# Second attention of a two-layer encoder: two heads turned in one transpose, rows spread by DMA

## The reference

```python
q, k, v = jnp.split(h @ w_in, 3, axis=-1)          # 16 heads of 64
q = rmsnorm(q.reshape(B, S, N_HEADS, HEAD_DIM), q_g)
k = rmsnorm(k.reshape(B, S, N_HEADS, HEAD_DIM), k_g)
# every chunk of 64 queries sees its own chunk and the 8 before it
logits = jnp.einsum('bqhd,bkhd->bhqk', q_c, k_c) * scale + bias
logits = jnp.where(valid, logits, -jnp.inf)
p = jax.nn.softmax(logits, axis=-1)
o = jnp.einsum('bhqk,bkhd->bqhd', p, v_c)
h = h + m @ w_out
```

## Time and profile before

| | us |
|---|---|
| median of 3 runs | 2830.57 |
| lowest, highest | 2827.06, 2833.55 |
| profiled execution, its own time | 2832.51 |
| span in its trace | 2830.7 |
| busy in the span: PE, PEld | 2737.7, 2378.0 |
| busy in the span: DVE, ACT, POOL | 1406.7, 1124.8, 952.1 |
| unit loop of the second attention | 1727 to 1996 in the trace |

### The profile page before, as it was taken

The page is one execution under the profiler, slowest core; times in us unless marked ns, Lnnn a source line. Parts: engine busy times, 40 slices in busy tenths (PEclk is TensorE's granted clock), DMA queues, the critical chain, the costliest instruction groups (busy, mean ns, idle before and its releaser), DMA issues. The chain is left out here.

```text
span 2830.7 us, 38924 instructions
## 1 busy us (share of the span) xinstructions
PE 2737.7 (97%) x14678; PEld 2378.0 (84%) x14678; DVE 1406.7 (50%) x2300; ACT 1124.8 (40%) x2409; POOL 952.1 (34%) x695
## 2 busy tenths in 40 slices
PE   7799999999999999999999999999989999999999
PEld 6599889887788888888889998989868888888887
DVE  5888766631544444445441114656244544444444
ACT  5677666642322222222245556777223222222221
POOL 2124433102332233222344445665133233232222
PEclk9899999999999999999999999999999999999999
DMA  5100000101111111111121100002111111111111
GB/s 173 45 26 21 27 9 9 64 24 51 47 55 50 44 44 52 52 44 44 52 93 52 61 23 7 28 13 81 31 53 51 45 44 52 51 45 51 44 52 60
DMA packets 38756, 132.44 MB, mean 47 GB/s; under 512 B 4240, under 2 KB 12608, under 8 KB 36960
## 3 DMA queue, kind: packets, MB, share of 16 engines
q1 hardware_dynamic: 38624, 130.68, 14.1%
HBM read 122.22 MB, written 13.69 MB: 48 GB/s over the span
## 5 line engine op out<-in xcount | busy, mean ns | idle before, releaser
L367 PE MATMUL banks<-XH,WH 128*128 128x512 f32 x1408 | 440.8, 394 | 19.2 <-POOL WL L314 12.6
L314 POOL TENSOR_TENSOR WL<-WR,WH 128x1024 fp32r<-128x1024 f32 x132 | 330.0, 2507 | 380.7 <-ACT WH L260 380.7
L367 PE MATMUL banks<-XL,WH 128*128 128x512 f32 x1408 | 441.2, 395 | 0.0
L367 PE MATMUL banks<-XH,WL 128*128 128x512 f32 x1408 | 438.3, 393 | 0.0
L275 ACT ACTIVATE Y<-U,CONVB,CONVW 128x1024 f32<-128x1024 f32 x88 | 109.5, 1244 | 639.8 <-DVE U L415 639.8
L367 PEld LDWEIGHTS banks<-XH,WH 128*128 128x128 f32 x1408 | 265.3, 189 | 78.9 <-POOL WL L314 13.4
L367 PEld LDWEIGHTS banks<-XH,WL 128*128 128x128 f32 x1408 | 266.1, 189 | 60.9
L415 DVE TENSOR_TENSOR U<-banks,RB 128x1024 f32<-128x1024 f32 x88 | 107.8, 1225 | 418.4 <-PE banks L367 403.5
L367 PEld LDWEIGHTS banks<-XL,WH 128*128 128x128 f32 x1408 | 266.2, 189 | 58.1
L322 POOL TENSOR_TENSOR AL<-Y,AH 128x1024 fp32r<-128x1024 f32 x44 | 106.2, 2413 | 611.8 <-ACT AH L283 611.8
L405 DVE TENSOR_TENSOR XT<-XT,banks 128x1024 f32<-128x1024 f32 x176 | 214.6, 1219 | 164.5 <-PE banks L383 164.5
(11 more groups left out here) (257 smaller groups left out, 5535.2 us busy)
## 6 DMA issues: line engine op xcount, KB each, us to landing
WR<-in_ffn SPq DMA_DIRECT2D x132, 512.0 KB, 3.5
QWR<-in_qkv SPq DMA_DIRECT2D x8, 1536.0 KB, 6.5
XT<-in_xT SPq DMA_DIRECT2D x16, 512.0 KB, 7.5
OWR<-in_w_o SPq DMA_DIRECT2D x16, 512.0 KB, 3.4
QWR1F<-in_qkv SPq DMA_DIRECT2D x4, 1536.0 KB, 6.6
spill<-XT SPq DMA_DIRECT2D x8, 512.0 KB, 10.8
XT<-spill SPq DMA_DIRECT2D x8, 512.0 KB, 7.1
outT<-XT SPq DMA_DIRECT2D x8, 512.0 KB, 2.6
```

Source lines behind the costliest of these rows:

```text
L314: pool.tensor_tensor(WL[:, ch % RING, :], WR[:, ch % RING, :], WH[:, ch % RING, :].bitcast(F32), ALU.subtract).then_inc(w_lo, 1)
L367: mm = pe.matmul(u[:, h * HALF:(h + 1) * HALF], w[:, ch % RING, db * P:(db + 1) * P], x[:, db, h * HALF:(h + 1) * HALF], start=(db == 0 an ...
```

## The change

Two heads are turned by one transpose of their natural 128 columns (q pair, k pair), so TQ holds head 0 in partitions 0 to 63 and head 1 in 64 to 127. ACT copies these 2 x 128 columns to a new buffer HC. Four DMAs per tile, issued by SP, bring each head's 64 rows into both halves of HT. POOL's split waits for the DMAs; its doubling is gone for the 56 tiles of the loop (tiles 0 to 7 keep it). ACT's copy of a tile waits for the DMAs of the tile two before.

```diff
@@ band_phase
+        HC = u.take("HC1", [P, 2, 2 * PAIR], F32)
...
-        q_copied, tq_free, out_high = sem("q_copied"), sem("tq_free"), sem("out_high")
+        h_landed = [sem("h_even"), sem("h_odd")]
+        tq_free, out_high = sem("tq_free"), sem("out_high")
@@ sync
+            def spread(t):
+
+                n, pairs = t - TT, HT[:, t % 2, :].rearrange("p (b h n) -> p b h n", b=2, h=2)
+                if n >= 2:
+                    sp.wait_ge(k_ready, n - 1)
+                sp.wait_ge(tq_free, round_of_tile(t) - TT + 1)
+                for h in range(2):
+                    head = HC[h * HD:(h + 1) * HD, t % 2, :].rearrange("p (b n) -> p b n", b=2)
+                    for to in range(2):
+                        sp.dma_start(pairs[to * HD:(to + 1) * HD, :, h, :], head).then_inc(h_landed[t % 2], 16)
+
+            for t in range(TT, 2 * TT):
+                spread(t)
             for k in range(2, GROUPS):
                 sp.wait_ge(max_done, UNITS * (k - 1))
                 sp.dma_start(BB[:, k % 2, :, PW - W:PW], near[k]).then_inc(b_landed[k % 2], 16)
...
                     for ch in range(c.chunks[1].count):
                         sp.dma_start(c.chunks[1].W[:, ch, :], stream[ch]).then_inc(c.chunks[1].landed, 16)
+                for t in range(k * TT, (k + 1) * TT):
+                    spread(t)
@@ scalar
             def heads_copy(t, r):
                 act.wait_ge(turned, r + 1)
-                if t >= TT + 2:
-                    act.wait_ge(k_ready, t - TT - 1)
-                act.activation(HT[:, t % 2, 0:2 * P], TQ[:, 0:2 * P], ACT.Copy, scale=c.HGAIN[:, 2:3]).then_inc(q_copied, 1)
-                act.activation(HT[:, t % 2, 2 * P:4 * P], TQ[:, 2 * P:4 * P], ACT.Copy,
+                n = t - TT
+                if n >= 2:
+                    act.wait_ge(h_landed[t % 2], 64 * (n // 2))
+                act.activation(HC[:, t % 2, 0:PAIR], TQ[:, 0:PAIR], ACT.Copy, scale=c.HGAIN[:, 2:3])
+                act.activation(HC[:, t % 2, PAIR:2 * PAIR], TQ[:, PAIR:2 * PAIR], ACT.Copy,
                                scale=c.HGAIN[:, 3:4]).then_inc(tq_free, 1)
@@ gpsimd
-                pool.wait_ge(q_copied, n + 1)
+                pool.wait_ge(h_landed[t % 2], 64 * (n // 2 + 1))
...
-                pool.wait_ge(tq_free, round_of_tile(t) - TT + 1)
...
-            doubled(TT)
-            doubled(TT + 1)
...
                     split(t)
-                    if t + 2 < TILES:
-                        doubled(t + 2)
@@ tensor
+            def heads_compact(t, r):
+                pe.wait_ge(normed, t + 1)
+                wait_seat(r)
+                for j in range(2):
+                    mm = pe.transpose(TQ[:, j * PAIR:(j + 1) * PAIR], tile(t)[:, j * PAIR:(j + 1) * PAIR], c.IDF[:])
+                mm.then_inc(turned, 1)
...
-                    heads(tile_of(g), rounds_before(g))
+                    heads_compact(tile_of(g), rounds_before(g))
```

## The result

The changed kernel takes **2837.57 us** (median of 12 runs, 2831.86 to 2842.44), the kernel before, run beside it, 2831.05 us (12 runs, 2827.06 to 2833.99). The ratio is 1.0025, 95% interval 1.0017 to 1.0032: slower by 6.5 us, where 6.4 us less was forecast; 2837.57 lies above the range of 2810 to 2834. The profiled execution took 2842.44 us (the slowest of the twelve; span 2840.6, clock 0.985), that of before 2832.51 (span 2830.7, clock 0.990).

The account below looks back on a forecast made before the run. TensorE, busy 262.4 of 269 us, was taken to bound the second attention's unit loop. Terms -12.9 - 4.5 - 2.0 + 13.0 = -6.4 us gave 2824.2 us against a median of 2830.6; range 2810 to 2834.

Parts of the forecast that it names:

- A: Likeliest case: gains less one group 7 stall, as one queue's last transfers wait for the first; 2824.2 us, chance 0.54.
- transposes: Second attention's unit loop: two transposes fewer per tile, 0.23 us for each of 56 tiles, -12.9 us.
- group 4's burst: Before group 4, BB and two OWR, a quarter of the bytes, make rows land about when due: 0.
- group 7's stall: TensorE waits for late rows in group 7: 10.9 us, restart 0.5, lower clock 1.6, together +13.0 us.
- bank waits and late doubling: Loop: output transpose's waits for the TQ bank, -4.5 us; transposes at 1905.85 late for POOL's doubled rows, -2.0 us.
- ACT's copies: Copies shrink from 256 to 128 columns, a pair taking 0.47 instead of 0.84 us, freeing TQ earlier: -4.5 us.
- The DMAs at price 0: Each loop tile's four row transfers land about 3.5 us after the copies, soon enough for POOL's split: price 0.
- Rival D: Four DMAs served one after the other, landing after 6.8 to 10.4 us, set the loop's pace: 2859 us, chance 0.08.
- The place where it costs: Before group 7, tile 56's rows queue behind BB, XT and WR; TensorE stalls at an output transpose: +10.9 us.
- The clock: After group 7's stall the granted clock stays low, priced from the idle stretch around 1728 to 1730: +1.6 us.
- Rival B: Tile 56's transfers slip past the load or it drains faster: only the gain remains, 2811.2 us, chance 0.16.
- rival C: DVE and ACT set the pace in short units, savings come back as other waits: 2830.7 us, chance 0.18.

Follow-up runs that it names:

- no_spread: The changed kernel without HC and the row DMAs, ACT copying into HT, rows not reaching both halves (output not the reference's): 2812.64 us, ratio 0.9938 to before.
- load_behind: The changed kernel with the eight XT and two WR transfers issued behind group 7's tiles instead of ahead: 2820.63 us, ratio 0.9969 to before.
- half_dmas: The changed kernel with only the two DMAs per tile that cross halves, own-half rows left out (output not the reference's): 2828.48 us, ratio 1.0001 to before.
- three_deep: The changed kernel with three buffers of HT and HC instead of two, all four DMAs per tile kept: 2826.61 us, ratio 0.9984 to before.

## Why the prediction was wrong

The mechanism forecast as the likeliest case, A, is the one that happened: the transposes are saved, the DMAs of rows are free in an undisturbed group, and the load ahead of tile 56's rows makes one large stall. The sign was wrong, because the terms of the sum were mis-sized, all in one direction: above all group 4's burst, put at 0 and worth 5.3 us, and group 7's stall with its clock, put at 13.0 and measured at 18.75. Forecast -6.4 us, measured in the loop +8.1:

| term | forecast | measured |
|---|---|---|
| transposes | -12.9 | -12.3 (0.22 a tile, 56 tiles) |
| bank waits and late doubling | -6.5 | -4.5 (the rest of no_spread's 16.8) |
| group 7's stall, restart and clock | +13.0 | +18.75 |
| group 4's burst | 0 | +5.3 |
| start of the loop and the rest | not named | +0.8 |
| sum | -6.4 | +8.1 |

*Transposes.* 0.24 us a pair against 0.46 for four: right to within 0.01 us. All work of an undisturbed group became 2.15 us shorter.

*Start of the loop.* From the last doubled turn to tile 15's the changed kernel took 34.32 us and load_behind, the same code there, 33.72: this term is scatter between executions, not a cost of the change.

*ACT's copies.* The step that took 0.47 us for the pair by the 279 ns of another copy was off: 0.6 us. The bank waits went from 5.0 to 2.0 us, so their part was -3.0, not -4.5. The late doubling at 1905.85 is gone: no wait of its kind stands at group 6.

*The DMAs at price 0.* Right, in all groups without a burst, and no_spread shows it (30.95 us in both). Rival D falls: the four transfers overlap. SP issues them some 0.7 us apart, and each of the 224 lands after a median of 2.0 us:

```profile
HT<-HC SPq DMA_DIRECT2D x224, 64.0 KB, 2.0
```

```profile
1950.98 2.54 SPq L661 DMA_DIRECT2D HT<-HC  x4
```

These are tile 58's four; the last is issued at 1952.91 and the landing takes 2.0 us, so all are there 4 us after the first issue, where paying 2.0 us four times over would have needed 8. That working of the forecast's, four times the fixed cost, is what the trace refutes. By the Trainium skill, DMA: Bandwidth & Descriptors, Rules for kernel authors, the parts over the two halves serialize; whether their bytes are moved one after the other no run here tells, since at this load's 5.6 MB per 17.3 us 64 KB take 0.2 us (an estimate), less than the 0.6 between two issues. The fixed cost of some 2.0 us, which the forecast took from the same page's anatomy of one DMA, is given there for transfers that GpSimd issues; SP's here land after a median of 2.0.

*"The place where it costs".* This step named the right place and the right chain and was too small in nearly every link:

```profile
1923.86 2.85 SPq L661 DMA_DIRECT2D HT<-HC  x4
1926.75 0.59 SPq L667 DMA_DIRECT2D BB<-near  x1
1927.44 4.05 SPq L676 DMA_DIRECT2D XT<-spill  x8
1931.53 1.73 SPq L678 DMA_DIRECT2D WR<-in_ffn  x2
1933.36 4.61 SPq L661 DMA_DIRECT2D HT<-HC  x5
```

| us, after tile 55's turn (T55, 1922.72) | forecast | measured |
|---|---|---|
| copies done | 0.90 | 1.07 |
| four issues of tile 55 | 1.5 | 2.85 |
| BB issued | 2.53 | 4.03 |
| from BB to tile 56's rows landed | 18.1 | 21.7 |
| rows landed | 20.6 | 25.7 |
| TensorE at the output transpose | 10.2 | 10.8 |

"Four issues of 0.38" came from the issues of loads out of HBM; an issue of this SBUF-to-SBUF form takes about 0.7 us. "Tile 56's 0.26 MB add 0.8" was right: the rows landed 0.8 us behind the second WR transfer. What was late was that transfer itself, 20.8 us after BB's issue and not 17.3 to 17.6 as in the three other traces under half_dmas. The stretch ahead of the landing shows how:

```profile
1946.00:1948.00 2.00, 0.00 (x0) 0.00 (x0) 0.00 (x0) 0.00 (x0) 0.00 (x0) 0.50 0.07 23
```

The engines' mean busy share had fallen from 1.05 (1944.5 to 1945) to 0.09 (1945.5 to 1946) and is 0.07 here, about that of one in sixteen (an estimate). Why that one ran some 3 us longer stays open; three_deep, with the same order of transfers, doesn't show it. So of the chain the slower issues (BB 1.5 us later than forecast) belong to the change, and some 3.3 us may belong to this execution. The forecast's 0.04 for "about 2838, if small pieces are slow" came near the measured 2837.57 by number, and for a reason that holds in part only: their issue is slow, their landing behind the load isn't. The stall was 15.64 us instead of 10.9, and ACT's copy of tile 58 was released by the DMA as foretold (order of time on ACT):

```profile
1948.51 0.37 ACT L721 ACTIVATE HC<-banks,HGAIN 128x128 f32<-128x128 f32 x1 [16.51 <-DMA HT<-HC]
1948.78 0.36 ACT L722 ACTIVATE HC<-banks,HGAIN 128x128 f32<-128x128 f32 x1
```

*The clock.* 1.6 us was the price taken from the loop's start. After the 15.64 us without a matmul the granted clock stayed at the lower level for some 6.0 us more (stretches by stage, columns as above):

```profile
1943.00:1945.00 2.00, 0.00 (x0) 0.00 (x0) 0.00 (x0) 0.00 (x0) 0.00 (x0) 0.50 1.15 252
...
1949.00:1951.00 2.00, 1.81 (x8) 1.60 (x9) 0.58 (x3) 1.64 (x6) 1.86 (x4) 0.50 0.00 0
...
1953.00:1955.00 2.00, 2.00 (x12) 2.00 (x11) 1.19 (x3) 1.13 (x4) 0.38 (x2) 0.50 0.35 90
1955.00:1956.00 1.00, 1.00 (x7) 0.96 (x8) 0.00 (x0) 0.69 (x2) 0.92 (x2) 0.92 0.25 65
1956.00:1958.00 2.00, 2.00 (x18) 1.94 (x18) 1.47 (x5) 1.18 (x3) 1.32 (x3) 1.00 0.40 101
```

12 matmul records in 2 us at 0.50 and 18 at 1.00: about 3 us lost, with 15.64 the 18.75 of the term.

*Group 4's "0".* "A quarter of it, so about when the copy is due" was a proportion laid upon a time that isn't one. What counts is lateness beyond the slack: here that left 3.23 us of stall, and a clock of 0.73 and 0.81 over the next 7.5 us, some 1.7 us more. This term alone would have turned -6.4 into -1.1; the stall's size, 5.75 us, and the smaller savings, 2.6 us, did the rest. One whole row of the table above, group 4's, was never worked out, only waved at by scale.

Rival B (no stall) and rival C (the saving isn't kept) fall too: the stall is there, and no_spread keeps 16.8 of 19.4 us.

## What to carry to other kernels

Before a small, latency-bound DMA goes on a queue, list the bulk loads on that queue and on the DMA engines at the same time: its landing is late by what is queued ahead of it, and the buffers between it and TensorE cover only their own depth. Put the bulk load where no small transfer follows, or one piece at a time between them; here another queue removed 3 of the 18.75 us (POOL's own standstill counted in), and one buffer more all of group 4's 5.3 but only 5.7 of the 18.75. And work out every such place in the same steps, in microseconds of lateness against slack, instead of scaling the result of one to the next.

## What the runs showed of the hardware that was not expected

- An ACT copy of 128 columns over 64 partitions takes as long as over 128 (362 and 367 ns), and the scaled copy 367 ns where the copy into XH, unscaled and to another type, takes 279.
- SP's issue of a 64 KB SBUF-to-SBUF transfer with 512 B pieces takes some 0.6 to 0.7 us (four in 2.85), of BB 0.59 in the same stretch, of an XT load 0.51.
- A tile's DMA lands in a median of 2.0 us; with a 5.6 MB load ahead in its queue after up to 12.6, beside the load in another queue after up to 8.6.
- Of the sixteen DMA engines about one was still busy (share 0.07) from 1946 to 1948 in the changed kernel's execution, and the second WR transfer and tile 56's last rows landed only at its end.
- POOL's issues stopped for 10.37 us after seven transfers of 512 KB. The profile names only "issue"; what it waited for stays open.
